# VectorE makes the sum S3 behind the last pair's first gate and S4 behind its last scaling, in place of the other order

## The chip, the core and the metric

One core of one Trainium2 chip runs the kernel. The metric is the device time of one execution in microseconds (us). The engines are TensorE (PE in the profile, PEld its weight loads), VectorE (DVE), ScalarE (ACT), GpSimd (POOL) and SyncE (SP), which issues the DMA transfers of weights.

## The reference, cut to what matters

A trunk of two layers (`DEPTH` 2), width 1024, 512 tokens, all in float32. Each layer mixes tokens and then runs a convolutional feed-forward block, which is where the change lies:

```
h = rmsnorm(x, g_ffn[l])
z = dwconv_centred(h @ w_up[l], conv_w[l], conv_b[l])      # three taps along the tokens
z_gate, z_val = split(z, [D_FF])                            # D_FF = 2816
x = x + (silu(z_gate) * z_val) @ w_down[l]
```

## The kernel before, in words

**Float32 products in three passes.** Every weight slab (128 x 1024, one of a ring of four slots `raw(0)` to `raw(3)`) is split in two: ScalarE writes its high part `w_hi` (a Copy into fp32r), and GpSimd then subtracts it from the slab and writes the low part `w_lo` (`low`, L397 to L399). A product is then three matmuls: high by high, high by low, low by high.

**The feed-forward block** goes through the 22 tiles of D_FF in parts: two full parts of 8 tiles and a last one of 6, in each of the two layers. In a full part the up projection makes two tiles (a pair) in each of four stages, k = 0 to 3 (`up_pair`). TensorE projects four slabs (gate and value of two tiles, accumulators 0 to 3); VectorE multiplies each with the rms scale (`scale(0)` to `scale(3)`, L1204), ScalarE makes the middle tap (`centre`, L738), VectorE adds the two outer taps (`taps`, L1213), ScalarE takes silu, and VectorE gates (`gate`, L1220). ScalarE and VectorE also split the gated tile into high and low parts.

**The down projection of a full part** is done in two quads of four output tiles each, by a Winograd form of Strassen's product: seven products ("units") of half size in place of eight. It needs sums of the weight quarters beside the quarters themselves: S1 = raw(1) + raw(3), S2 = S1 - raw(0), S4 = raw(2) - S2, and S3 = raw(0) - raw(1), which is written over raw(1). It also needs sums T1 to T4 of the activations (`t1` to `t4` in `up_pair`, L1238 to L1251). In the last pair stage (k = 3) of a full part the first quad's weights are prepared: GpSimd makes S1 and S2 (L410, L412), VectorE makes S4 and S3. There are four such stages in the program: two full parts in each of two layers.

**The order around the change** is written out by hand, one instruction stream for each engine, which runs in order, with semaphores between:

- VectorE, stage k = 3: ..., `gate(0)`, S4 (L1232, waits for S2 by `sum_done_pool`), `scale(2)` (L1204), the low part of the even tile (L1235), t1 (L1238), `taps(1, 0)`, the low part of t1 (L1241), `scale(3)`, S3 (L1244), `taps(1, 1)`, `gate(1)`, t2, t4, t3 (L1248 to L1251). Then `down_quads`: it adds unit 1's product to x (`add_unit`, L1264), splits the odd tile and the t's (`odd_low`, L1188 and L1190), adds unit 2, makes the second quad's sums (L1278 to L1290) and adds the other units. Each sum counts up `sum_done`, and the consumers wait for a count and not for a name.
- ScalarE, stage k = 3 (`unit_hi`, L726): high parts of raw(0), S1, S2, raw(2), then `centre(1, 1)`, then S3 (raw(1)) into slot 0, after a wait for unit 1 and for `sum_done`. Then the odd tile and the t's (L791, L792), and in `down_quads` S4 into slot 1 and raw(3).
- GpSimd (`low_quads`, L401 to L424): low(raw(0)), S1, S2, low(S1), then a wait for the high part of S2 and for `sum_done` 6m + 2 (both sums), low(S2), low(raw(2)), low(S3), low(S4), low(raw(3)), and the second quad's seven. With m counting the full parts, `sum_done` rises by six in each.
- TensorE (`down_quads`, L1718 on; matmuls at L1696, L1698, L1699; a unit of all four pairs is 24 matmuls of 256 columns): unit 1, raw(0) by the even tile, into bank 0; unit 2, S1 by T1, into bank 1; the first half of raw(2) by the odd tile (12 matmuls, bank 2), which waits for low(raw(2)) by `lo_sum` 6m + 3; then S2 by T2 into bank 0, which waits for low(S2) and for `unit_added` 6m + 1, that is until VectorE has added unit 1 out of bank 0; its last pair waits for the t's low parts (`t_ready`); the second half of raw(2) by the odd tile; then S4 by the odd tile into bank 1, which waits for low(S4); S3 by T3; raw(3) by T4; and the second quad.
- SyncE reloads raw(0) with the second quad's slab once low(S2) is done (`lo_done`), raw(2) once low(S4) is done. The loads of raw(1) and raw(3) of the second quad went earlier, into other memory.

Of the kernel before, what the change touches and what calls it, by code (L numbers as in the profile page):

```python
# [41 lines left out]
RING = 4  # L42
# [31 lines left out]
def encoder(nc, xT, slabs, rank_w, gate_w, gate_b, spatial_w, spatial_b, ln_gb, gains, gla_gain, conv, consts, outT):  # L74
    with ExitStack() as ctx:
# [187 lines left out]
        def raw(j):  # L263
            return w_raw[:, j * SLAB:(j + 1) * SLAB]
# [107 lines left out]
        @block.gpsimd  # L372
        def _(pool):

            pool.memset(ones, 1.0).then_inc(ones_set, 1)
            pool.memset(eps[:, :], EPS).then_inc(lo_done, RING)
            for j, part in ((0, 0), (1, 0), (0, 1), (1, 1), (0, 2), (1, 2)):
                w = slice(j * SLAB + W_PARTS[part].start, j * SLAB + W_PARTS[part].stop)
                if part < 2:
                    pool.wait_ge(hi_part[j], part + 1)  # L380
                else:
                    pool.wait_ge(hi_done, j + 1)
                pool.tensor_tensor(w_lo[:, w], w_raw[:, w], w_hi[:, w].bitcast(F32),
                                   ALU.subtract).then_inc(lo_part[j] if part < 2 else lo_done, 1)
            pool.wait_ge(xg_ready, KT)
            for j in (2, 3):
                w = slice(j * SLAB, (j + 1) * SLAB)
                pool.wait_ge(hi_done, j + 1)
                pool.tensor_tensor(w_lo[:, w], w_raw[:, w], w_hi[:, w].bitcast(F32),  # L389
                                   ALU.subtract).then_inc(lo_done, 1)  # L390
            def low_slabs(L, first, end):
                with pool.Fori(L * (NS // RING) + first // RING, L * (NS // RING) + end // RING) as q:
                    for j in range(RING):
                        pool.wait_ge(hi_done, q * RING + (j + 1))
                        low(j, raw(j)).then_inc(lo_done, 1)

            def low(slot_of, source):  # L397
                w = slice(slot_of * SLAB, (slot_of + 1) * SLAB)
                return pool.tensor_tensor(w_lo[:, w], source, w_hi[:, w].bitcast(F32), ALU.subtract)  # L399

            def low_quads(L, part):  # L401
                m, slab = quads_at(L, part)
                n = L * NS + slab
                pool.wait_ge(hi_sum, 6 * m + 1)
                low(0, raw(0)).then_inc(lo_sum, 1)
                pool.wait_ge(raw_loaded[1], 16 * (n // RING) + 16)
                pool.wait_ge(raw_loaded[3], 16 * (n // RING) + 16)
                if m:
                    pool.wait_ge(sum_done, 6 * m)
                pool.tensor_tensor(sum_s1, raw(1), raw(3), ALU.add).then_inc(sum_done_pool, 1)  # L410
                pool.wait_ge(sum_done_pool, 2 * m + 1)
                pool.tensor_tensor(sum_s2[:, :], sum_s1, raw(0), ALU.subtract).then_inc(sum_done_pool, 1)  # L412
                pool.wait_ge(hi_sum, 6 * m + 2)
                low(1, sum_s1).then_inc(lo_sum, 1)
                pool.wait_ge(hi_done, n + 1)
                pool.wait_ge(sum_done, 6 * m + 2)
                low(2, sum_s2[:, :]).then_inc(lo_done, 1)
                pool.wait_ge(hi_sum, 6 * m + 3)
                low(3, raw(2)).then_inc(lo_sum, 1)
                pool.wait_ge(hi_done, n + 2)  # L420
                low(0, raw(1)).then_inc(lo_done, 1)
                pool.wait_ge(hi_done, n + 3)
                low(1, sum_s4).then_inc(lo_done, 1)
                pool.wait_ge(hi_done, n + 4)  # L424
                low(2, raw(3)).then_inc(lo_done, 1)

                pool.wait_ge(hi_sum, 6 * m + 4)
                low(3, raw(0)).then_inc(lo_sum, 1)
                pool.wait_ge(hi_sum, 6 * m + 5)
                low(1, sum_s1).then_inc(lo_sum, 1)  # L430
                pool.wait_ge(hi_sum, 6 * m + 6)
                low(0, raw(2)).then_inc(lo_sum, 1)
                pool.wait_ge(hi_done, n + 5)
                pool.wait_ge(sum_done, 6 * m + 6)
                low(2, sum_s2[:, :]).then_inc(lo_done, 1)
                pool.wait_ge(hi_done, n + 6)
                low(3, second_raw[1]).then_inc(lo_done, 1)
                pool.wait_ge(hi_done, n + 7)
                low(1, sum_s4).then_inc(lo_done, 1)
                pool.wait_ge(hi_done, n + 8)  # L440
                low(2, second_raw[3]).then_inc(lo_done, 1)

            for L in range(DEPTH):
                before = RING if L == 0 else 0
                for part in range(FULL_PARTS):
                    low_slabs(L, before, N_FFN + part * PART + 2 * KT)
                    low_quads(L, part)
                    before = N_FFN + (part + 1) * PART
                low_slabs(L, before, NS)
# [3 lines left out]
        def _(act):  # L453
# [91 lines left out]
            with act.Fori(0, DEPTH) as L:  # L545
# [179 lines left out]
                def unit_hi(slot_of, source, done):  # L725
                    act.activation(w_hi[:, slot_of * SLAB:(slot_of + 1) * SLAB], source, ACT.Copy).then_inc(done, 1)  # L726

                def up_pair(slab, tile, stage, even, odd, t_of, down=None):
# [49 lines left out]
                    if down is None:  # L778
                        centre(1, 1)
                        next_hi(3)  # L780
                    else:
                        act.wait_ge(acc_ready, L * NS + slab + RING)
                        raw_at(2, first)
                        unit_hi(3, raw(2), hi_sum)
                        centre(1, 1)
                        act.wait_ge(unit_done, 14 * m + 1)
                        act.wait_ge(sum_done, 6 * m + 2)
                        unit_hi(0, raw(1), hi_done)
                    act.wait_ge(t_done, stage * 2 + 2)
                    on_its_own(act)  # L790
# [3 lines left out]
                def down_quads(part):  # L794
                    m, slab = quads_at(L, part)
                    act.wait_ge(unit_done, 14 * m + 2)
                    unit_hi(1, sum_s4, hi_done)
                    act.wait_ge(unit_done, 14 * m + 3)
                    unit_hi(2, raw(3), hi_done)

                    act.wait_ge(unit_done, 14 * m + 4)
                    raw_at(0, slab + RING)
                    unit_hi(3, raw(0), hi_sum)
                    act.wait_ge(unit_done, 14 * m + 5)
                    act.wait_ge(sum_done, 6 * m + 3)
                    unit_hi(1, sum_s1, hi_sum)
                    act.wait_ge(unit_done, 14 * m + 6)
                    raw_at(2, slab + RING)
                    unit_hi(0, raw(2), hi_sum)
                    act.wait_ge(unit_done, 14 * m + 7)  # L810
                    act.wait_ge(sum_done, 6 * m + 5)
                    unit_hi(2, sum_s2[:, :], hi_done)
                    act.wait_ge(unit_done, 14 * m + 8)
                    unit_hi(3, second_raw[1], hi_done)
                    act.wait_ge(unit_done, 14 * m + 9)
                    act.wait_ge(sum_done, 6 * m + 6)
                    unit_hi(1, sum_s4, hi_done)
                    act.wait_ge(unit_done, 14 * m + 10)
                    act.wait_ge(second_loaded[3], 16 * m + 16)
                    unit_hi(2, second_raw[3], hi_done)  # L820

                    act.wait_ge(unit_done, 14 * m + 11)
                    raw_at(0, slab + 2 * RING)
                    split_hi(0)
                    act.wait_ge(unit_done, 14 * m + 13)
                    raw_at(1, slab + 2 * RING)
                    split_hi(1)
                    act.wait_ge(unit_done, 14 * m + 14)
                    raw_at(2, slab + 2 * RING)
                    split_hi(2)  # L830
                    raw_at(3, slab + 2 * RING)
                    split_hi(3)
# [60 lines left out]
        def _(dve):  # L893
# [49 lines left out]
            with dve.Fori(0, DEPTH) as L:  # L943
# [249 lines left out]
                def up_pair(part, k):  # L1193
# [34 lines left out]
                    gate(0)  # L1228
                    if k == KP - 1:
                        dve.wait_ge(sum_done_pool, 2 * m + 2)  # L1230
                        dve.wait_ge(raw_loaded[2], 16 * (L * (NS // RING)) + 4 * first + 16)
                        dve.tensor_tensor(sum_s4, raw(2), sum_s2[:, :], ALU.subtract).then_inc(sum_done, 1)  # L1232
                    scale(2)
                    dve.wait_ge(feat_hi_done, L * NF + part * KT + (KT + 2 * k + 1))
                    dve.tensor_tensor(lo(0, H), gated[0][:, 0:H], hi(0, H).bitcast(F32),  # L1235
# [5 lines left out]
                    dve.tensor_tensor(lo(H, H), t1, hi(H, H).bitcast(F32), ALU.subtract).then_inc(t_ready, 1)  # L1241
                    scale(3)
                    if k == KP - 1:
                        dve.tensor_tensor(raw(1), raw(0), raw(1), ALU.subtract).then_inc(sum_done, 1)  # L1244
                    taps(1, 1)
                    gate(1)
                    dve.wait_ge(gated_done, f + 2)
# [680 lines left out]
```

## Time and profile before

| | us |
|---|---|
| median of 3 runs | 1109.97 (1109.26 to 1110.15) |
| the profiled execution, its own time | 1112.22 |
| its span in the trace | 1110.3 |
| TensorE busy | 1090.2 |
| VectorE busy | 666.3 |
| ScalarE busy | 516.4 |
| GpSimd busy | 553.8 |

The mean granted clock of TensorE over the span is 0.989 of full speed. The span is what the trace covers; the execution's own time is 1.9 us more. In the rows, a time is the start in us from the span's beginning and the second number is the duration; x2 are two like instructions merged. The record of a GpSimd or VectorE instruction covers the time from its issue to its end, waits inside the instruction included; waits for a semaphore stand as idle time before it. A row of windows has its length, the busy time and count of PE, PEld, DVE, ACT and POOL, TensorE's granted clock as a share of full speed (PEclk), and the DMA share and GB/s.

### The profile page before, as it was taken

The page shows a single profiled execution, that of the slowest core. Times are in us where ns is not written, and L with a number is a line of the kernel's source. Part 1 is how long each engine was busy: PE and PEld are TensorE (multiplying, and loading weights), DVE is VectorE, ACT ScalarE, POOL GpSimd, SP SyncE. Part 2 cuts the span into 40 slices and gives each one's busy share as a digit, 9 for nine tenths or more (in the row PEclk, how much of TensorE's full clock was granted, in tenths as well). Part 3 has the DMA queues.
Part 4 walks back from the last instruction along what each step waited for, and adds up shares of the span by engine and source line. Part 5 has one row for each costly group of instructions (what it writes and reads, how often), then busy time and mean ns, then how long its engine had stood idle before and what let it go on. Part 6 is the DMA issues. An engine that isn't in the chain of part 4 may idle for free.

```text
span 1110.3 us, 17568 instructions
## 1 busy us (share of the span) xinstructions
PE 1090.2 (98%) x5904; PEld 932.7 (84%) x5904; DVE 666.3 (60%) x960; ACT 516.4 (47%) x720; POOL 553.8 (50%) x234
## 2 busy tenths in 40 slices
PE   9999999999899999999999999999989999899997
PEld 7788888888898889888878888888879888898887
DVE  5726755677826777355636368467776377744545
ACT  7835444454434443344557344355443444333441
POOL 5333244345774459644634333334468544685450
PEclk9999999999999999999999999999999999899999
DMA  8222222232142221423522221223322423133222
GB/s 306 86 95 78 76 76 96 78 112 94 40 152 95 94 76 57 152 95 98 178 97 94 78 77 58 95 76 106 103 76 72 138 95 118 46 101 115 95 76 76
DMA packets 33620, 108.96 MB, mean 98 GB/s; under 512 B 3984, under 2 KB 6800, under 8 KB 33552
## 3 DMA queue, kind: packets, MB, share of 16 engines
q1 hardware_dynamic: 32848, 107.03, 29.1%
q10 hardware_dynamic: 704, 1.07, 0.3%
q8 instruction: 38, 0.62, 0.2%
q14 instruction: 30, 0.25, 0.1%
HBM read 105.98 MB, written 2.10 MB: 97 GB/s over the span
## 4 chain that ended last, share of the span: by engine, by line
issue 48%; POOL 32%; PE 14%; DVE 2%; ACT 1%; DMA 1%; POOLq 1%; DVEq 0%; SPq 0%; ACTq 0%
POOL w_lo L399 30%; PE acc L1385 3%; PE acc L1386 3%; PE acc L1387 3%; PE acc L1696 2%; PE acc L1699 2%; PE acc L1698 2%; POOL sum_s L412 1%; POOL mixer_sb L410 1%; DMA x<-xT 1%; DVE arena L1213 1%; DVE arena L1360 1%; DVE side L1204 1%; DVE w_raw L1244 0%; POOL w_lo L389 0%
## 5 line engine op out<-in xcount | busy, mean ns | idle before, releaser
L399 POOL TENSOR_TENSOR w_lo<-w_raw,w_hi 128x1024 fp32r<-128x1024 f32 x180 | 441.0, 2455 | 492.3 <-ACT w_hi L457 468.4
L1385 PE MATMUL acc<-xg_hi,w_hi 128*128 128x512 f32 x864 | 338.9, 392 | 0.0
L1386 PE MATMUL acc<-xg_lo,w_hi 128*128 128x512 f32 x864 | 336.3, 389 | 0.0
L1387 PE MATMUL acc<-xg_hi,w_lo 128*128 128x512 f32 x864 | 336.2, 389 | 0.0
L457 ACT ACTIVATE w_hi<-w_raw 128x1024 fp32r<-128x1024 f32 x158 | 166.7, 1059 | 163.8 <-PE acc L1387 94.7
L1385 PEld LDWEIGHTS acc<-xg_hi,w_hi 128*128 128x128 f32 x864 | 162.2, 188 | 35.6 <-issue 2.0
L1387 PEld LDWEIGHTS acc<-xg_hi,w_lo 128*128 128x128 f32 x864 | 162.2, 188 | 34.0
L1386 PEld LDWEIGHTS acc<-xg_lo,w_hi 128*128 128x128 f32 x864 | 162.3, 188 | 33.3 <-issue 0.5
L1213 DVE SCALAR_TENSOR_TENSOR arena<-side,conv_sb,arena 128x511 f32<-128x511 f32 x128 | 95.9, 749 | 64.8 <-ACT arena L738 54.0
L1385 PE MATMUL acc<-feat_hi,w_hi 128*128 128x512 f32 (+1 forms) x236 | 89.3, 379 | 0.0
L1386 PE MATMUL acc<-feat_lo,w_hi 128*128 128x512 f32 (+1 forms) x236 | 89.3, 378 | 0.0
L1387 PE MATMUL acc<-feat_hi,w_lo 128*128 128x512 f32 (+1 forms) x236 | 89.3, 378 | 0.0
L1696 PE MATMUL acc<-feat_hi,w_hi 128*128 128x256 f32 x256 | 74.4, 291 | 12.2 <-POOL w_lo L399 12.2
L738 ACT ACTIVATE arena<-side,conv_sb 128x512 f32<-128x512 f32 x64 | 49.7, 777 | 74.4 <-DVE side L1204 73.3
L1264 DVE TENSOR_TENSOR x<-x,acc 128x512 f32<-128x512 f32 (+1 forms) x56 | 40.4, 721 | 64.7 <-PE acc L1699 64.7
L1699 PE MATMUL acc<-feat_hi,w_lo 128*128 128x256 f32 x256 | 74.0, 289 | 0.0
L1698 PE MATMUL acc<-feat_lo,w_hi 128*128 128x256 f32 x256 | 73.9, 289 | 0.0
L1696 PEld LDWEIGHTS acc<-feat_hi,w_hi 128*128 128x128 f32 x256 | 50.4, 197 | 13.1 <-POOL w_lo L399 13.0
L1204 DVE TENSOR_TENSOR side<-acc,rstdT 128x512 f32<-128x512 f32 x64 | 44.4, 693 | 27.2 <-PE acc L1387 25.6
L898 DVE SCALAR_TENSOR_TENSOR xg_lo<-x,gains_sb,xg_hi 128x512 fp32r<-128x512 f32 x32 | 40.7, 1280 | 30.0 <-ACT xg_hi L466 29.9
L1696 PE MATMUL acc<-t_hi,w_hi 128*128 128x256 f32 x192 | 57.0, 297 | 0.1
L1698 PE MATMUL acc<-t_lo,w_hi 128*128 128x256 f32 x192 | 56.5, 295 | 0.0
(177 smaller groups left out, 1734.0 us busy)
## 6 DMA issues: line engine op xcount, KB each, us to landing
w_raw<-slabs SPq DMA_DIRECT2D x182, 512.0 KB, 3.3
arena<-slabs SPq DMA_DIRECT2D x8, 512.0 KB, 5.0
outT<-arena SPq DMA_DIRECT2D x7, 256.0 KB, 2.2
mixer_sb<-ln_gb SPq DMA_DIRECT2D x2, 512.0 KB, 7.0
w_raw<-slabs SPq DMA_DIRECT2D x4, 128.0 KB, 4.3
x<-xT ACTq DMA_DIRECT2D x2, 256.0 KB, 4.4
x<-xT SPq DMA_DIRECT2D x2, 256.0 KB, 5.7
x<-xT ACTq DMA_DIRECT2D x1, 512.0 KB, 6.7
```

The source lines that it names most:

```text
L399: return pool.tensor_tensor(w_lo[:, w], source, w_hi[:, w].bitcast(F32), ALU.subtract)
L457: act.activation(w_hi[:, w], w_raw[:, w], ACT.Copy).then_inc(hi_done, 1)
L738: act.activation(z[j], y[j], ACT.Identity, scale=conv_sb[:, bass.ds(coef + 1, 1)], bias=conv_sb[:, bass.ds(coef + 3, 1)]).then_inc(centre_ ...
L898: dve.scalar_tensor_tensor(out=xg_lo[:, w], in0=x[:, w], scalar=gains_sb[:, bass.ds(r * KT + m, 1)], in1=xg_hi[:, w].bitcast(F32), op0=ALU ...
L1204: dve.tensor_tensor(y[j], acc[j][:, :], rstdT[:, :], ALU.mult).then_inc(y_ready, 1)
L1213: dve.scalar_tensor_tensor(out=to, in0=of, scalar=conv_sb[:, bass.ds(coef + tap, 1)], in1=to, op0=ALU.mult, op1=ALU.add).then_inc(taps_don ...
L1385: pe.matmul(out, wh, ah, start=first, stop=False)
L1386: pe.matmul(out, wh, al, start=False, stop=False)
L1387: return pe.matmul(out, wl, ah, start=False, stop=last)
L1696: pe.matmul(out, w_hi[:, a:a + P], xh, start=(first and k == 0 and r == 0), stop=False, skip_group_check=True)
L1698: pe.matmul(out, w_hi[:, a:a + P], xl, start=False, stop=False, skip_group_check=True)
L1699: last = pe.matmul(out, w_lo[:, a:a + P], xh, start=False, stop=(k == KP - 1), skip_group_check=True)
```

## The change

The two sums of the first quad change places on VectorE, and the counts that others wait for follow:

```diff
@@ GpSimd, low_quads
                 pool.wait_ge(hi_done, n + 1)
-                pool.wait_ge(sum_done, 6 * m + 2)
+                pool.wait_ge(sum_done, 6 * m + 1)
                 low(2, sum_s2[:, :]).then_inc(lo_done, 1)
@@ ScalarE, up_pair
                         act.wait_ge(unit_done, 14 * m + 1)
-                        act.wait_ge(sum_done, 6 * m + 2)
+                        act.wait_ge(sum_done, 6 * m + 1)
                         unit_hi(0, raw(1), hi_done)
@@ ScalarE, down_quads
                     act.wait_ge(unit_done, 14 * m + 2)
+                    act.wait_ge(sum_done, 6 * m + 2)
                     unit_hi(1, sum_s4, hi_done)
@@ VectorE, up_pair
                     gate(0)
                     if k == KP - 1:
                         dve.wait_ge(sum_done_pool, 2 * m + 2)
-                        dve.wait_ge(raw_loaded[2], 16 * (L * (NS // RING)) + 4 * first + 16)
-                        dve.tensor_tensor(sum_s4, raw(2), sum_s2[:, :], ALU.subtract).then_inc(sum_done, 1)
+                        dve.tensor_tensor(raw(1), raw(0), raw(1), ALU.subtract).then_inc(sum_done, 1)
                     scale(2)
...
                     scale(3)
                     if k == KP - 1:
-                        dve.tensor_tensor(raw(1), raw(0), raw(1), ALU.subtract).then_inc(sum_done, 1)
+                        dve.wait_ge(raw_loaded[2], 16 * (L * (NS // RING)) + 4 * first + 16)
+                        dve.tensor_tensor(sum_s4, raw(2), sum_s2[:, :], ALU.subtract).then_inc(sum_done, 1)
                     taps(1, 1)
                     gate(1)
```

GpSimd's wait before low(S2) stands for S3 alone after the change: raw(0) is free to be loaded again once S3 has read it.

## Rows read from the trace of the kernel before

**Rows 1.** The page of the profile, busy time of each engine over the span.
```profile
PE 1090.2 (98%) x5904; PEld 932.7 (84%) x5904; DVE 666.3 (60%) x960; ACT 516.4 (47%) x720; POOL 553.8 (50%) x234
```

**Rows 2.** The waits of all engines: who waited for whom, us in total, times, longest.
```profile
PE acc L1696 <- POOL w_lo L399: 12.2, 4, 3.3
...
DVE arena L1213 <- DVE arena L1213: 2.1, 8, 0.5
```

**Rows 3.** Timeline of POOL at the first quads: start us, us, what, idle before.
```profile
271.95 2.39 POOL L399 TENSOR_TENSOR w_lo<-mixer_sb,w_hi 128x1024 fp32r<-128x1024 f32 x1
281.37 2.39 POOL L399 TENSOR_TENSOR w_lo<-sum_s,w_hi 128x1024 fp32r<-128x1024 f32 x1 [7.03 <-DVE w_raw L1244]
283.71 4.71 POOL L399 TENSOR_TENSOR w_lo<-w_raw,w_hi 128x1024 fp32r<-128x1024 f32 x2
288.36 3.12 POOL L399 TENSOR_TENSOR w_lo<-mixer_sb,w_hi 128x1024 fp32r<-128x1024 f32 x1
...
305.59 2.40 POOL L399 TENSOR_TENSOR w_lo<-sum_s,w_hi 128x1024 fp32r<-128x1024 f32 x1
```

**Rows 4.** Timeline of DVE, the same stretch.
```profile
272.25 3.17 DVE L1232 TENSOR_TENSOR mixer_sb<-w_raw,sum_s 128x1024 f32<-128x1024 f32 x1 [1.28 <-POOL sum_s L412]
...
279.06 0.43 DVE L1241 TENSOR_TENSOR feat_lo<-arena,feat_hi 128x256 fp32r<-128x256 f32 x1
279.40 0.69 DVE L1204 TENSOR_TENSOR side<-acc,rstdT 128x512 f32<-128x512 f32 x1
280.00 1.22 DVE L1244 TENSOR_TENSOR w_raw<-w_raw 128x1024 f32<-128x1024 f32 x1
281.35 0.75 DVE L1213 SCALAR_TENSOR_TENSOR arena<-side,conv_sb,arena 128x511 f32<-128x511 f32 x1
...
285.32 0.68 DVE L1264 TENSOR_TENSOR x<-x,acc 128x512 f32<-128x512 f32 x1
...
286.89 2.34 DVE L1190 TENSOR_TENSOR t_lo<-arena,t_hi 128x768 fp32r<-128x768 f32 x1
```

**Rows 5.** Timeline of ACT, the same stretch.
```profile
277.34 1.05 ACT L726 ACTIVATE w_hi<-sum_s 128x1024 fp32r<-128x1024 f32 x1
...
279.50 1.04 ACT L726 ACTIVATE w_hi<-w_raw 128x1024 fp32r<-128x1024 f32 x1
...
286.76 1.05 ACT L726 ACTIVATE w_hi<-mixer_sb 128x1024 fp32r<-128x1024 f32 x1
```

**Rows 6.** Timeline of PE, the same stretch.
```profile
280.12 0.28 PE L1696 MATMUL acc<-feat_hi,w_hi 128*128 128x256 f32 x1
...
282.88 0.28 PE L1699 MATMUL acc<-feat_hi,w_lo 128*128 128x256 f32 x1
286.12 0.38 PE L1696 MATMUL acc<-feat_hi,w_hi 128*128 128x256 f32 x1 [2.97 <-POOL w_lo L399]
...
288.27 0.41 PE L1696 MATMUL acc<-t_hi,w_hi 128*128 128x256 f32 x1
...
293.46 0.28 PE L1696 MATMUL acc<-feat_hi,w_hi 128*128 128x256 f32 x1
...
308.05 0.39 PE L1696 MATMUL acc<-t_hi,w_hi 128*128 128x256 f32 x1
```

**Rows 7.** Windows from TensorE's restart to its S4 unit; PEclk stands behind POOL's busy time.
```profile
286.12:293.46 7.34, 7.34 (x49) 7.34 (x50) 7.26 (x6) 2.74 (x4) 5.47 (x3) 0.77 0.18 51
...
830.57:838.97 8.40, 8.40 (x48) 8.40 (x49) 7.57 (x6) 2.76 (x4) 5.44 (x3) 0.65 0.25 87
...
sum 31.53, PE 31.48 PEld 31.48 DVE 29.80 ACT 10.24 POOL 21.87; mean PE 7.87 PEld 7.87 DVE 7.45 ACT 2.56 POOL 5.47
```

**Rows 8.** Timeline of DVE in an ordinary pair stage of layer 1.
```profile
798.43 2.09 DVE L1241 TENSOR_TENSOR feat_lo<-arena,feat_hi 128x256 fp32r<-128x256 f32 x1
```

**Rows 9.** Timeline of POOL, that same stage.
```profile
797.84 2.40 POOL L399 TENSOR_TENSOR w_lo<-w_raw,w_hi 128x1024 fp32r<-128x1024 f32 x1 [2.93 <-ACT w_hi L457]
```

**Rows 10.** All instructions of line L1241: duration ns min/median/max.
```profile
L1241 DVE TENSOR_TENSOR feat_lo<-arena,feat_hi x16: 424/2088/2109, 213.4 to 956.7; 128x256 fp32r<-128x256 f32 x16
```

## The prediction

> **What bounds the kernel now.** I read the page first: TensorE is busy for 1090.2 us of the span and no other engine comes near [rows 1], so only what makes TensorE stand still, or slows its clock, counts. The list of waits names one large stop that repeats: TensorE's L1696 waits for GpSimd's low parts, four times, 12.2 us in all [rows 2]. These are the four full parts, at the point that the diff touches. The timelines of the first of them, engine by engine, give the chain; the other three show the same order.
>
> TensorE begins unit 2 at 280.12 and issues its last matmul at 282.88, so 24 matmuls take 2.88 us, 0.12 each. It restarts at 286.12 with raw(2) by the odd tile, begins S2 by T2 at 288.27 and S4 by the odd tile at 293.46 [rows 6]. The restart waits for low(raw(2)), the first of the two GpSimd instructions that begin at 283.71; it stands behind low(S2), which began at 281.37 after 7.03 us of idleness that S3 ended [rows 3]. S3 ran on VectorE from 280.00 to 281.22 [rows 4]. The high part of S2 was there from 278.39 (277.34 + 1.05), that of raw(2) from 280.54 [rows 5]. So GpSimd stood still for 3 us for S3 alone.
>
> Behind each stop the clock is low for a while. From restart to the S4 unit TensorE issues 48 matmuls, 5.76 us at 0.12. The first window is 7.34 us at a mean clock of 0.77, the third 8.40 us at 0.65; the four sum to 31.53 [rows 7]. The half clock (1.2 for 2.4 GHz) thus costs 31.53 - 4 x 5.76 = 8.5 us, 1.6 us in two of the parts and 2.6 in the others.
>
> **The change, part by part** (first full part; the others take the same steps).
>
> *S3 moves forward.* It takes S4's place at 272.25. S4 there took 3.17 us [rows 4], since GpSimd's low(S1), 271.95 to 274.34 [rows 3], lay beside it: the S4 record ends at 275.42, which is 274.34 + 1.08. S3 alone takes 1.22, of which some 1.08 is work, and has the same shape, so I cost it at the same 3.17 and `scale(2)` behind it does not move. Bounds: 1.22 and 3.17. Both are hidden, because TensorE is in its up slabs then.
>
> *GpSimd starts low(S2) earlier.* It is released by the high part at 278.39; the step from ScalarE to GpSimd is 0.07 or so, making 278.46 to 280.86 in place of 281.37. The new count asks for S3, which is long done.
>
> *What the earlier start collides with.* L1241 (the low part of t1) reads two SBUF operands, and in this stage it took only 0.43 us, with GpSimd idle [rows 4]. Over all 16 stages its median is 2088 ns, its least 424 [rows 10]. An ordinary stage shows why: GpSimd's instruction begins at 797.84 and ends at 800.24, L1241 begins 0.59 later and ends at 800.52, 0.28 behind it [rows 8, 9]. With low(S2) from 278.46 and L1241 from 279.06 the new stage has the same geometry, so L1241 ends at about 281.14, not 279.49. That is +1.65 for VectorE. It also holds unit 2 of TensorE, which needs that low part, from 280.12 to 281.2.
>
> *S4 moves behind `scale(3)`.* `scale(3)` (0.69, one operand in PSUM, never stretched) runs to 281.75. S4 wants to start at 281.65, but GpSimd has taken up low(raw(2)) at 281.14, and it needs 2.25 once it is free to run: the instruction that begins at 288.36 ends at 291.48, 2.25 behind the end (289.23) of the VectorE instruction that was ahead of it [rows 3, 4]. So low(raw(2)) ends at 283.40, and S4 at 283.40 + 1.08 = 284.48. S3 ended at 281.22 in this place: VectorE's tail is 3.26 us late. Bounds for S4: 1.22 if nothing stood in its way, the 3.17 of rows 4 at the most; worked out it is 2.83, and the latter is the nearer row, since there too GpSimd's instruction was under way.
>
> *What of TensorE's gains.* low(raw(2)) comes at 283.40 in place of 286.05. TensorE ends unit 2 at 281.2 + 2.88 = 284.08 and goes straight on with raw(2) by the odd tile, 12 matmuls, to 285.52. **Then it stops again**: S2 by T2 goes into bank 0 and waits until VectorE has added unit 1 out of it. That add stands behind `taps(1, 1)`, `gate(1)`, t2, t4, t3. Before, it ran 285.32 to 286.00, which was 2.27 before TensorE's S2 unit at 288.27 [rows 4, 6]. With the tail 3.26 late it ends at 289.26, and TensorE restarts at 289.33. The two taps had a gap of up to 0.5 us between them (eight gaps, 2.1 us in all [rows 2]); if that goes, 288.9. I take 289.15.
>
> *The rest of the way to the S4 unit* is 36 matmuls (S2 by T2, and the second half of raw(2)), 4.32 us and the clock's cost c. So S4's unit starts at 289.15 + 4.32 + c = 293.47 + c, and before it was 286.12 + 5.76 + c = 291.88 + c: **+1.6 us a part**, between +1.2 (288.9, the tap gap gone) and +1.8. The new stop, from 285.52 to 289.15, is 3.6 us for 3.1, so I expect no less of the low clock, and take the same 8.5 us for all four. Its ends: 1.6 in each part (6.4 in all) and 2.7 in each (10.8), the two values of rows 7, so -2.1 to +2.3 in all.
>
> *What must not be late behind it.* low(S3) is hidden. S4's high part moves with the odd tile's work on ScalarE, from 286.76 [rows 5] to about 289.8, and low(S4) from 288.36 to 291.0, ended at 293.3: in time for 293.47 + c, as c was never below 1.6. The t's low part (L1190, 2.34 before [rows 4]) finds GpSimd idle and takes about 1 us; it is there by 291.1, when the third pair of S2 by T2 is done. SyncE's reload of raw(0) starts earlier, that of raw(2) about 2 us later, needed only for the second quad's sums some 8 us on. Low parts of the second quad are close: low(S2) there ran 305.59 to 307.99 and TensorE's unit began at 308.05 [rows 3, 6]. Both move back together, so I cost it at nothing, and at 0.5 us a part if one more collision falls there.
>
> **Sum.** 4 x 1.6 = +6.4 us. Against the profiled execution that is 1112.22 + 6.4 = 1118.6, a span of 1116.7. The median of the runs shown is 1109.97, 2.25 below the profiled execution, and the forecast for the median is 1109.97 + 6.4 = 1116.4.
>
> **Rivals.**
>
> *The intended gain arrives (6%).* If L1241 and S4 ran beside GpSimd unhindered, VectorE's tail would stay where it is, the add would end at 286.00 and TensorE would go on at 286.07: 286.07 + 4.32 = 290.4 with a stop of 1.5 us and perhaps no low clock. Against 293.46 that is -3.1 a part, -12.3, about 1097.7. Against it stand rows 8 and 10. The Trainium skill, "Advanced Engine Details and Errata", section VectorE Performance Modes, says that VectorE's 2-port instructions and GpSimd's block each other, and names no others; by that, float32 subtractions would run free and 1097.7 would come out. The Trainium skill, "SBUF — State Buffer", section Who interferes with whom, says that a VectorE instruction with two SBUF inputs contends with a GpSimd one that reads SBUF, and that the first to issue holds the port to its end, which speaks against this change. By that one the sum above stands, and the trace agrees with it: 2.09 against 0.43 us for one and the same L1241.
>
> *S4 slips in ahead of low(raw(2)) (10%).* If GpSimd's queued instruction came second, S4 would end at 282.9, the tail would be 1.65 late, low(raw(2)) would end at 285.1, and TensorE would restart at 287.7: 292.0 + c, +0.1 a part, and from +0.5 us in all to -6 where the shorter stops (2 us) keep the clock up. 1104 to 1110.5. Against it: S4 is asked for half a microsecond after low(raw(2)) can start.
>
> *Slower by more (12%).* The late tail takes with it low(S4), by the ScalarE work between. Its place is the S4 unit; it decides if low(S4) ends behind 293.47 + c, that is if the tail is a further 1.8 us late, as by one more collision of L1190 with a 2.25 us GpSimd instruction. Then each part pays 1 us more, +10 to +11: 1120.5. Together with the clock at its dear value, 1122.
>
> *The change does nothing measurable (4%).* Only if TensorE's wait for bank 0 had as much slack as the tail loses; 2.27 us of slack against 3.26 says no, and the slack was itself the old stop.
>
> **Numbers.** The forecast's own case has 68%: +6.4, from 4 x 1.2 - 2.1 = +2.7 to 4 x 1.8 + 2.3 = +9.5. The range runs from 1111.5 (the lower end of that, with 1 us for an S4 that waits less) to 1121 (its upper end with part of the third rival). About 0.2% (2.2 us) is what a measurement of this kernel can tell from no change. Faster by more: 6% and half of the second rival's 10%, and a little, 0.11. Within: the other half, 4% of no effect, and the forecast's lower tail, 0.10. Slower: 0.79.
>
> **What would show it.** Right: GpSimd's idle time before low(S2) down from 7 to about 4 us and ended by ScalarE; L1241 in all 16 stages near 2.09; L1232 behind `scale(3)` at 2.8 us; L1244 at 3.2; TensorE's wait before L1696 no longer for GpSimd's low part but for VectorE's L1264, on the matmuls of t_hi, 3 to 4 us in each part, with a short one of 1 us before unit 2; low clock still there in all four. Wrong: L1241 at 0.43 with GpSimd running; S4 at 1.2 us; the add of unit 1 at 286; or a clock that no longer falls, which alone would give back 8.5 us and turn the sign.

## The result, and the profile after

The changed kernel takes 1117.49 us in the median of five runs (1114.22 to 1117.81), the kernel before 1109.97 (1109.26 to 1114.32, five runs). The ratio is 1.0056, with a 95% interval from 1.0032 to 1.008: slower by 3.6 to 8.9 us. The profiled execution took 1117.64 us with a span of 1115.9; against that of before it is 5.4 us more, and the span 5.6.

The list of who waited for whom, for TensorE, in the changed kernel (us in all, times, longest). Some lines stand one further on than before: L1697 is the old L1696, L1265 the add (L1264), L1205 a scaling (L1204), L1214 a tap (L1213), L1189 and L1191 the low parts of the odd tile and of the t's (L1188, L1190). L1232 is now S3, and L1245 the moved S4.

```profile
PE acc L1697 <- DVE x L1265: 13.0, 4, 3.4
PE acc L1697 <- DVE feat_lo L1241: 4.1, 4, 1.0
...
PE acc L1697 <- POOL w_lo L399: 0.5, 2, 0.3
```

Against [rows 2], the four waits of 12.2 us for GpSimd's low parts are gone. In their place stand four of 13.0 us for VectorE's add of unit 1 and four of 1.0 us for L1241. TensorE stops for longer than before, and for another engine.

GpSimd's timeline in the first full part, to be read against [rows 3]. The trace of after runs 0.1 us behind that of before at this point.

```profile
278.57 2.39 POOL L399 TENSOR_TENSOR w_lo<-sum_s,w_hi 128x1024 fp32r<-128x1024 f32 x1 [4.13 <-ACT w_hi L726]
280.92 2.57 POOL L399 TENSOR_TENSOR w_lo<-w_raw,w_hi 128x1024 fp32r<-128x1024 f32 x1
283.98 2.84 POOL L399 TENSOR_TENSOR w_lo<-w_raw,w_hi 128x1024 fp32r<-128x1024 f32 x1 [0.49 <-ACT w_hi L726]
291.02 2.37 POOL L399 TENSOR_TENSOR w_lo<-mixer_sb,w_hi 128x1024 fp32r<-128x1024 f32 x1 [4.21 <-ACT w_hi L726]
```

With the offset taken off, low(S2) starts 2.9 us earlier, behind ScalarE's high part, and low(raw(2)) ends at 283.5 in place of 286.05. That is what the diff changes for GpSimd, and it works. VectorE's timeline, against [rows 4]:

```profile
272.12 3.40 DVE L1232 TENSOR_TENSOR w_raw<-w_raw 128x1024 f32<-128x1024 f32 x1 [1.09 <-POOL sum_s L412]
...
279.16 2.07 DVE L1241 TENSOR_TENSOR feat_lo<-arena,feat_hi 128x256 fp32r<-128x256 f32 x1
281.16 0.69 DVE L1205 TENSOR_TENSOR side<-acc,rstdT 128x512 f32<-128x512 f32 x1
281.76 2.81 DVE L1245 TENSOR_TENSOR mixer_sb<-w_raw,sum_s 128x1024 f32<-128x1024 f32 x1
284.50 0.74 DVE L1214 SCALAR_TENSOR_TENSOR arena<-side,conv_sb,arena 128x511 f32<-128x511 f32 x1
...
288.46 0.68 DVE L1265 TENSOR_TENSOR x<-x,acc 128x512 f32<-128x512 f32 x1
...
290.03 0.96 DVE L1191 TENSOR_TENSOR t_lo<-arena,t_hi 128x768 fp32r<-128x768 f32 x1
```

L1241 takes 2.07 us, S4 2.81. Each of the two was asked for while a low part of GpSimd's was under way, and ends 0.3 and 1.1 us behind it (GpSimd's ends are 280.96 and 283.49). The add of unit 1 ends at 289.14, where it ended at 286.00. TensorE's restart, and then its S4 unit:

```profile
289.29 0.36 PE L1697 MATMUL acc<-t_hi,w_hi 128*128 128x256 f32 x1 [3.37 <-DVE x L1265]
...
295.17 0.28 PE L1697 MATMUL acc<-feat_hi,w_hi 128*128 128x256 f32 x1
```

The four windows from that restart to the S4 unit (the last row is their sum; PEclk stands behind POOL's busy time). They hold 36 matmuls, not the 48 of [rows 7].

```profile
289.29:295.17 5.88, 5.88 (x37) 5.88 (x37) 5.83 (x6) 2.72 (x3) 2.58 (x2) 0.71 0.12 18
...
970.72:977.33 6.61, 6.61 (x34) 6.61 (x35) 6.25 (x6) 2.71 (x3) 2.37 (x1) 0.56 0.19 55
sum 24.21, PE 24.20 PEld 24.21 DVE 23.70 ACT 10.86 POOL 9.91; mean PE 6.05 PEld 6.05 DVE 5.92 ACT 2.72 POOL 2.48
```

The half clock costs 24.21 - 4 x 4.32 = 6.9 us in these windows, against 8.5 in the profiled execution of before.

### The profile page after: what moved, and what is told of

It reads as the page before. It is cut to its first block, busy times and chain, and to the rows that moved or that the text cites. A ratio compares the mean times of both kernels' runs of the same rounds, so it can differ in the third digit from the quotient of the medians.

```text
span 1115.9 us, 17572 instructions
## 1 busy us (share of the span) xinstructions
PE 1090.3 (98%) x5904; PEld 932.0 (84%) x5904; DVE 676.5 (61%) x960; ACT 516.4 (46%) x720; POOL 554.8 (50%) x234
## 4 chain that ended last, share of the span: by engine, by line
issue 49%; POOL 31%; PE 13%; DVE 3%; ACT 2%; DMA 1%; POOLq 1%; DVEq 0%; SPq 0%; ACTq 0%
POOL w_lo L399 29%; PE acc L1388 3%; PE acc L1387 3%; PE acc L1386 3%; PE acc L1697 2%; PE acc L1699 1%; PE acc L1700 1%; DVE arena L1214 1%; POOL sum_s L412 1%; POOL mixer_sb L410 1%; DMA x<-xT 1%; ACT arena L738 1%; DVE arena L1361 1%; DVE side L1205 1%; POOL w_lo L389 0%
## 5 line engine op out<-in xcount | busy, mean ns | idle before, releaser
L1214 DVE SCALAR_TENSOR_TENSOR arena<-side,conv_sb,arena 128x511 f32<-128x511 f32 x128 | 95.9, 749 | 64.3 <-ACT arena L738 54.0
L1265 DVE TENSOR_TENSOR x<-x,acc 128x512 f32<-128x512 f32 (+1 forms) x56 | 40.3, 722 | 61.4 <-PE acc L1700 61.1
L1697 PE MATMUL acc<-feat_hi,w_hi 128*128 128x256 f32 x256 | 73.0, 285 | 4.1 <-DVE feat_lo L1241 4.1
L1697 PE MATMUL acc<-t_hi,w_hi 128*128 128x256 f32 x192 | 58.1, 303 | 13.6 <-DVE x L1265 13.0
L1205 DVE TENSOR_TENSOR side<-acc,rstdT 128x512 f32<-128x512 f32 x64 | 44.4, 693 | 27.1 <-PE acc L1388 25.5
L1700 PE MATMUL acc<-t_hi,w_lo 128*128 128x256 f32 x192 | 57.3, 299 | 0.0
```

The lines of the kernel that those rows point to most:

```text
L1205: dve.tensor_tensor(y[j], acc[j][:, :], rstdT[:, :], ALU.mult).then_inc(y_ready, 1)
L1214: dve.scalar_tensor_tensor(out=to, in0=of, scalar=conv_sb[:, bass.ds(coef + tap, 1)], in1=to, op0=ALU.mult, op1=ALU.add).then_inc(taps_don ...
L1697: pe.matmul(out, w_hi[:, a:a + P], xh, start=(first and k == 0 and r == 0), stop=False, skip_group_check=True)
L1700: last = pe.matmul(out, w_lo[:, a:a + P], xh, start=False, stop=(k == KP - 1), skip_group_check=True)
```

## The experiments

Two theories stood at the start. **Port**: L1241 and S4 have both operands in SBUF and wait while a low part of GpSimd's is under way; that makes VectorE's tail late, and TensorE waits for it. **Order**: the new order of the sums is itself what costs. All runs below are timed against the kernel before on the same chip; its medians there were 1109.85 to 1109.92 us, as good as its 1109.97 above. The changed kernel was not timed again beside them: where a run is compared with it, its 1117.49 us are meant. The cuts of diffs are against the changed kernel, or against the kernel before where that is said, and leave out edits that only move a count or a line.

**GpSimd waits for both sums again.**

```diff
 pool.wait_ge(hi_done, n + 1)
-pool.wait_ge(sum_done, 6 * m + 1)
+pool.wait_ge(sum_done, 6 * m + 2)
 low(2, sum_s2[:, :]).then_inc(lo_done, 1)
```

> The changed kernel with one edit: GpSimd waits for both sums again before low(S2), so the order on VectorE is the new one but GpSimd starts as late as before. Port theory (VectorE's L1241 and S4 are stretched because GpSimd is at work beside them, and that makes the tail late): L1241 back at 0.43 us, S4 at 1.22 us behind the second scaling, low(S2) from about 281.4, TensorE's stop of 3 us before raw(2) again, and the time of the kernel before, 1110 us within 2. Rival (the new order by itself costs, through the later S4): 1116 to 1118, as the changed kernel.

Measured: 1109.91 us, ratio to before 1.0006 (0.9996 to 1.0017). Two rows of its VectorE timeline, L1241 and S4:

```profile
278.95 0.43 DVE L1241 TENSOR_TENSOR feat_lo<-arena,feat_hi 128x256 fp32r<-128x256 f32 x1
...
279.89 1.22 DVE L1245 TENSOR_TENSOR mixer_sb<-w_raw,sum_s 128x1024 f32<-128x1024 f32 x1
```

With the new order and the old start of GpSimd, both instructions shrink to 0.43 and 1.22 us and the whole loss is gone. Order falls: the new order by itself costs nothing, and the loss comes with GpSimd's earlier start.

**The add of unit 1 ahead of S4.**

```diff
 scale(3)
 if k == KP - 1:
+    add_unit(0, 0, 0, 0, 14 * m + 1, unit_added)
     dve.wait_ge(raw_loaded[2], 16 * (L * (NS // RING)) + 4 * first + 16)
     dve.tensor_tensor(sum_s4, raw(2), sum_s2[:, :], ALU.subtract).then_inc(sum_done, 1)
...
-add_unit(0, 0, 0, 0, units + 1, unit_added)
```

> The changed kernel with the add of unit 1 moved ahead of S4 on VectorE, where it fits into the time that S4 waits for GpSimd. Tail theory (the add is only the first of several things that come late; the t's low part is next): TensorE starts S2 by T2 at about 285.7 and stops 3 us later in the same unit, before its last pair, for VectorE's low part of the t's (ends near 291.0); 0.4 us a part gained, 1114 to 1117. Rival (the bank alone holds TensorE): the stop goes and 3.4 us a part with it, about 1104 or less.

Measured: 1113.10 us, ratio to before 1.0029 (1.0018 to 1.004). TensorE's waits for VectorE:

```profile
PE acc L1698 <- DVE t_lo L1191: 10.5, 4, 2.6
PE acc L1698 <- DVE feat_lo L1241: 4.2, 4, 1.1
```

The stop moved, it did not go: TensorE now stops for the t's low part, which ends at 290.5. So the bank was only the first of the late things; the tail as a whole is late. (Two waits for GpSimd, 2.2 us in all, came up in second quads besides.) It gained 4.4 us where 0.5 to 3.5 was expected. Part of that is probably the clock: the profile has two stretches of half clock behind these stops where the changed kernel's has four, and of the runs with a mean clock of 0.999 the one of the changed kernel took 1114.22 us and the one of this kernel 1113.03, only 1.2 us less. That is one run of each, so the split stays open.

**S4 made by GpSimd**, in its idle time before low(S2), and no longer by VectorE (those who wait for S3 wait for both sums again, 6m + 2).

```diff
 low(1, sum_s1).then_inc(lo_sum, 1)
+pool.wait_ge(sum_done_pool, 2 * m + 2)
+pool.wait_ge(raw_loaded[2], 16 * (n // RING) + 16)
+pool.tensor_tensor(sum_s4, raw(2), sum_s2[:, :], ALU.subtract).then_inc(sum_done, 1)
 pool.wait_ge(hi_done, n + 1)
-pool.wait_ge(sum_done, 6 * m + 1)
+pool.wait_ge(sum_done, 6 * m + 2)
```

> The changed kernel with S4 made by GpSimd behind low(S1), where GpSimd is idle for 4 us, and no longer by VectorE. Port theory: S4 on GpSimd takes 2.4 us (some 1 us more if it waits for S3 on the port), low(S2) still starts at about 278.6, L1241 still 2.09; VectorE's taps start at about 283.0 when the centre tap is ready and not at 284.5, the add of unit 1 ends near 287.3, TensorE stops for 1.8 us in place of 3.4: 1.9 us a part less, 1110; 1103 if the shorter stop keeps the clock at full speed. Rival (S4's 2.8 us on VectorE is not on the path): 1116 to 1118.

Measured: 1107.63 us, ratio to before 0.9978 (0.9969 to 0.9986), with no half clock behind the stops. Its TensorE waits:

```profile
PE acc L1697 <- DVE x L1265: 6.5, 4, 1.6
PE acc L1697 <- DVE feat_lo L1244: 4.0, 4, 1.0
PE acc L1697 <- POOL w_lo L399: 3.9, 4, 1.0
```

The first line halved as the port theory has it, and the clock stayed up, and yet the time is 1107.6 and not 1103. The third line says where the rest went: a stop of 1.0 us in each *second* quad, where GpSimd's chain of low parts is now the bound. Between 289.8 and 302.9 each of VectorE's four sums meets a low part and takes some 2.9 us:

```profile
289.83 3.01 DVE L1279 TENSOR_TENSOR mixer_sb<-arena 128x1024 f32<-128x1024 f32 x1
...
293.36 2.83 DVE L1282 TENSOR_TENSOR arena<-w_raw,arena 128x1024 f32<-128x1024 f32 x1
```

**Both edits together.** 

> Both edits: S4 on GpSimd, and the add of unit 1 right behind the second scaling, while the centre tap is awaited. Tail theory: S2 by T2 starts at 285.7 without a wait, and TensorE stops before its last pair until about 289.2 (1.4 us); the S4 unit starts near 291.4 in place of 295.2: about 1101 with the clock at full speed behind these short stops, 1108 if it still falls. Rival (bank or port are not what binds): no faster than the S4-on-GpSimd kernel alone.

Measured: 1108.55 us, ratio to before 0.9987 (0.9978 to 0.9995). The stop for the add went (6.5 us to none), one of 5.8 for the t's low part came, and the waits for GpSimd rose to 4.3. No gain beside the run before, but 0.9 us more: the rival named the right outcome. What fits it is that the second quad's chain of low parts sets the time by now, which the next run tests.

**S4's high part earlier on ScalarE**, on top of S4 on GpSimd.

```diff
 unit_hi(0, raw(1), hi_done)
+act.wait_ge(unit_done, 14 * m + 2)
+unit_hi(1, sum_s4, hi_done)
...
-act.wait_ge(unit_done, 14 * m + 2)
-act.wait_ge(sum_done, 6 * m + 2)
-unit_hi(1, sum_s4, hi_done)
```

> The kernel with S4 on GpSimd, and on ScalarE the high part of S4 moved ahead of the odd tile's work (behind a wait for unit 2), so that GpSimd makes low(S4) right behind low(S3), at about 286.4. The kernel with S4 on GpSimd stops 1 us in each second quad, since GpSimd meets four VectorE sums on the port there. Theory: with low(S4) gone from 289.4, the second quad's first sum (L1279) finds GpSimd idle and takes 1.2 us for 3.0, the chain of low parts to low(S2) of the second quad ends 1 us sooner, and that stop goes: about 1103.6. Rival (the chain starts no earlier and keeps its length, since it waits for raw(3)'s high part): 1107.6 as without the edit.

Measured: 1104.58 us, ratio 0.9938 (0.9921 to 0.9955). The second quad's first sum finds GpSimd idle, and TensorE's waits for low parts fall from 3.9 to 0.9 us:

```profile
290.02 1.21 DVE L1278 TENSOR_TENSOR mixer_sb<-arena 128x1024 f32<-128x1024 f32 x1
```

**Slab 3's scaling ahead of L1241**, on top of that.

```diff
+if k == KP - 1:
+    scale(3)
 dve.wait_ge(t_hi_done, stage * 2 + 1)
 dve.tensor_tensor(lo(H, H), t1, hi(H, H).bitcast(F32), ALU.subtract).then_inc(t_ready, 1)
-scale(3)
+if k < KP - 1:
+    scale(3)
```

> As the kernel before it in this call, and in the last pair stage the scaling of slab 3 goes ahead of L1241 on VectorE, so that the 1.65 us that L1241 loses to low(S2) no longer holds the centre tap. Port theory: L1241 still ends with low(S2) near 281.1 and TensorE's 1 us stop before unit 2 stays, but taps start at 281.3 for 283.1, the add of unit 1 ends near 285.6, and the stop before S2 by T2 (1.6 us) goes: about 1.6 us a part less, 1097. Rival (GpSimd's chain in the second quad is the bound by now): 1102 to 1104.

Measured: 1102.21 us, ratio 0.9916 (0.9899 to 0.9934), a miss by 5 us and inside the rival's range, though not for the rival's reason: TensorE's waits for GpSimd were 0.8 us in all. The stop for the add went as expected, but the t's low part (2.20 us, stretched behind low(S4)) came in its place with 3.3 us, and 4.1 us for L1241 stayed.

**TensorE's stop filled**, in the changed kernel (shown) and, in its stop behind unit 2, in the one before: 28 and 24 matmuls that nothing reads.

```diff
+pe.wait_ge(y_ready, ys + 4)
+for _ in range(28):
+    pe.matmul(acc[3][:, 0:H], feat_hi[:, 0:P], feat_hi[:, 0:H], start=True, stop=True, skip_group_check=True)
 pe.wait_ge(lo_done, n + 1)
 pe.wait_ge(unit_added, 6 * m + 1)
```

> The changed kernel with 28 matmuls of 256 columns (3.36 us) that nothing reads, into bank 3, in TensorE's stop of 3.65 us before S2 by T2. Theory of the clock (the stop costs its length, and the half clock behind it as much as 1.6 to 2.3 us a part more): S2 by T2 starts where it did, no half clock behind it, about 6.9 us less, 1110.6. Rival (the half clock is hidden, as other engines set the pace behind the stop): 1117.

> The kernel before with 24 such matmuls (2.88 us) in its stop of 3.1 us behind unit 2. Theory of the clock: 8.5 us less than the profiled run of before showed, 1101.5 to 1103. Rival (hidden): 1110.

Measured: 1114.45 us (ratio 1.0028, 1.0017 to 1.0039) and 1107.83 us (0.9972, 0.996 to 0.9984). No half clock is left behind the stops in either. But the gains are 3.0 and 2.1 us, not 6.9 and 8.5, and neither the theory's forecasts nor the rival's came out. For the kernel before, the 8.5 us are not the right measure: its profiled execution, at a mean clock of 0.989 and 1112.22 us, had more half clock than its usual run, at 0.993 to 0.996. The first experiment has the same stop as the kernel before and was profiled at 0.994. There the four windows of [rows 7] sum to 27.73 us, so the half clock takes 27.73 - 4 x 5.76 = 4.7 us, and the third part has none of it. So the fair pairs are 2.1 of 4.7 us for the usual runs, 1112.22 - 1108.04 = 4.2 of 8.5 us for the two profiled executions, and 3.0 of 6.9 us for the changed kernel: about half each time. The one run of the changed kernel that had a mean clock of 0.999 without any filling took 1114.22 us, as the filled one does. In the filled kernel before, TensorE waits for GpSimd again, for the most part in the second quads:

```profile
PE acc L1696 <- POOL w_lo L399: 4.0, 7, 0.8
```

The profiled execution of before has no such wait behind its four stops. In the changed kernel the same waits rise from 0.5 to 3.9 us by the filling. So about half of what the clock gives back is lost to GpSimd's chain of low parts; at half clock TensorE is late enough not to wait for it.

**One wait added to the changed kernel.** GpSimd lets L1241 pass before it starts low(S2).

```diff
 pool.wait_ge(sum_done, 6 * m + 1)
+pool.wait_ge(t_ready, 2 * KP * (m + 1) - 1)
 low(2, sum_s2[:, :]).then_inc(lo_done, 1)
```

> The changed kernel with one wait more: GpSimd starts low(S2) only when L1241 of this stage is done. Port theory: an added wait makes it faster. L1241 takes 0.43 us, low(S2) runs 279.6 to 281.95, S4 (asked for at 280.1) ends at 283.0 and not 284.5, low(raw(2)) ends near 285.3, the add of unit 1 near 287.8, and TensorE restarts with S2 by T2 near 287.9 for 289.3: about 1.4 us a part less, 1111 to 1113. Rival (GpSimd's low parts set TensorE's pace there, so that holding them back costs): 1118 or more.

Measured: 1109.23 us, ratio to before 0.9992 (0.9984 to 1.0001), so 8 us faster than the changed kernel, by waiting longer, and no faster than the kernel before. L1241 and S4:

```profile
279.65 0.42 DVE L1242 TENSOR_TENSOR feat_lo<-arena,feat_hi 128x256 fp32r<-128x256 f32 x1
...
280.59 3.15 DVE L1246 TENSOR_TENSOR mixer_sb<-w_raw,sum_s 128x1024 f32<-128x1024 f32 x1
```

It came out 2 us better than the range. In its trace low(raw(2)) ran behind S4 and ended at 286.0, and TensorE stopped for that, which hid the late add (in three of the four parts; in the third it still waited 0.8 us for it). Three stretches of half clock were left, of 2.6 to 3.2 us, where the changed kernel has four, three of 2.8 to 3.2 us and one of 5.3. How the 2 us divide between the two was not tested.

**The same wait, with S4 on GpSimd and its high part early.** 

> S4 on GpSimd and its high part early, and GpSimd yielding to L1241 as in the kernel before it in this call. Port theory: TensorE's stop before unit 2 (1.0 us) goes and one of about 1.3 us before raw(2) by the odd tile comes; the add of unit 1 ends near 285.8; then it depends on who asks first, L1191's low part of the t's (near 286.9) or low(S4) (near 286.7): 1104 to 1105 if low(S4) holds the port, 1100 if not. Rival (yielding only shifts the stop): 1104.6 as without it.

Measured: 1100.75 us, ratio 0.9912 (0.9898 to 0.9926). The t's low part asked before low(S4) (at 286.45, and it took 1.06 us):

```profile
PE acc L1697 <- POOL w_lo L399: 8.5, 8, 1.3
```

Nothing of VectorE holds TensorE any more; two short stops for low parts are left in each full part.

**The second quad's S3 earlier**, on top of the 1102 us kernel, without the added wait.

```diff
 dve.tensor_tensor(sum_s1, second_raw[1], second_raw[3], ALU.add).then_inc(sum_done, 1)
-add_unit(0, 0, 1, 0, units + 3, unit_added)
 dve.wait_ge(raw_loaded[0], loads)
+dve.wait_ge(sum_done, 6 * m + 3)
 dve.tensor_tensor(second_raw[1], raw(0), second_raw[1], ALU.subtract).then_inc(sum_done, 1)
+add_unit(0, 0, 1, 0, units + 3, unit_added)
```

> The 1102 us kernel (S4 on GpSimd, its high part early, scaling of slab 3 ahead of L1241) with the second quad's S3 made right behind its S1 on VectorE, before the add of S2 by T2, while GpSimd is idle. Theory: that sum then starts at 290.8, ahead of GpSimd's next low part at 291.4, and takes 1.2 us for 3.4; GpSimd's chain in the second quad loses only half a microsecond there, so TensorE's waits for it (0.8 us in all) go: 1101.2 to 1102. Rival (no change): 1102.2, since the stops before unit 2 and before the t's low part (7.4 us in all) are elsewhere.

Measured: 1100.86 us, ratio 0.9913 (0.9899 to 0.9928). That sum takes 1.23 us and TensorE's waits for GpSimd's low parts in the full parts are gone, as expected; those for VectorE's (4.1 us for t1's low part, 3.3 for the t's) stay:

```profile
290.88 1.23 DVE L1284 TENSOR_TENSOR arena<-w_raw,arena 128x1024 f32<-128x1024 f32 x1
```

These last two beat both kernels, by 9 us the one before and by over 16 the changed one. Their gain is made of work taken off VectorE's late tail and of collisions avoided.

## Why the prediction was right

The forecast was 1116.4 with 1111.5 to 1121; measured was 1117.5. Point by point, by its own steps, in the first full part (0.1 us taken off for the trace's offset):

- *S3 in S4's place costs nothing.* Right: it is stretched to 3.40 (3.17 forecast; it starts 0.2 earlier and ends at the same point), and `scale(2)` behind it does not move.
- *low(S2) from 278.46.* 278.47.
- *L1241 ends at 281.14.* 281.13. TensorE waits 1.0 us for it and starts unit 2 at 281.28 (281.2 forecast; 280.12 before). Over all 16 stages L1241's least is now 2072 ns.
- *S4 2.83 us, ending at 284.48.* 2.81, ending at 284.47.
- *TensorE restarts at 289.15* (between 288.9 and 289.33). 289.19. I had halved the gap between the two taps; in this part it stayed at 0.5, and in the second it was 0.27. With the gap whole my sum gives 289.33. It was 0.14 too late, because I took the tail to be as late as S4's end (3.26 us), but before the change the first tap began 0.13 behind S3's end and now it begins 0.07 before S4's record ends, so the taps, and the add with them, are only 3.0 us late. The two small errors nearly cancelled: that much is luck.
- *+1.6 us a part to the S4 unit, without the clock.* The S4 units start at 295.17, 429.00, 842.58 and 977.33, before at 293.46, 426.15, 838.98 and 972.13: 5.2 us later by the fourth. The clock's part of that is 6.9 - 8.5 = -1.6 us. The trace's offset (0.1) and TensorE's two waits for low parts in second quads (0.5, below) are in it too. That leaves 5.2 + 1.6 - 0.1 - 0.5 = 6.2 us, 1.55 a part.
- *low(S4) in time, from 288.36 to 291.0 and ended at 293.3.* 290.92 to 293.29, ahead of the S4 unit at 295.07.
- *The half clock, 8.5 us as before.* 6.9, inside the -2.1 to +2.3 stated, and there in all four parts of the profile; one of the five timed runs, with a mean clock of 0.999, can have had next to none.
- *The second quad's low parts at nothing.* TensorE waited for them twice, 0.5 us in all, both before the fourth S4 unit. The span is 5.6 us longer; the 0.4 us that come behind that unit stand in no wait that the list names.

In the profiles the difference is thus 5.4 (1117.64 - 1112.22) for the 6.4 forecast: 6.2 for the four parts, 1.6 less by the clock, 0.5 more by the second quads' waits, and a rest of 0.3. In the medians it is 7.5. That gap has a cause that I had not seen. The kernel before has 71 runs timed beside the experiments: 54 have a mean granted clock of 0.993 to 0.996 and take 1108.9 to 1110.7 us, 8 have 0.989 and take 1111.9 to 1112.5, 9 have 0.986 and 1113.7 to 1114.1. The profiled execution of before, with 0.989, is of the middle kind, and its 8.5 us of half clock are more than a usual run has. The changed kernel has 0.990 or 0.991 in four of its five runs, and 0.999 in the fifth, which took 1114.22. So where I took the clock's cost of the profiled execution over to both, the usual run before had less of it: 4.7 us by the first experiment's profile, where the changed kernel's profile has 6.9. With the half clock out of the way in both kernels (the two filled ones) the difference is 1114.45 - 1107.83 = 6.6 us, near the forecast's +6.4. So the mechanism and its price are right, and the term for the clock, zero in my sum, is what was mis-sized: -1.6 us between the two profiles, and in the medians some 1 us the other way (an estimate: half of 6.9 - 4.7, as half of it was lost above).

The Trainium skill, "SBUF — State Buffer", section Who interferes with whom, has the rule that decided it: a VectorE instruction with two SBUF inputs contends with a GpSimd one that reads SBUF, and the order of issue decides who blocks. The traces agree with it: the same L1241 takes 0.43 us beside an idle GpSimd and 2.07 beside a busy one, and whichever asks first goes first. The narrower statement that I had set against it, that of the Trainium skill, "Advanced Engine Details and Errata", section VectorE Performance Modes, gave 1097.7, and lost. The contention works the other way round too: low(S3), asked for at 283.98 while S4 was under way, took 2.84 us and not 2.4.

What one cannot read off the experiments is whether an S4 that slips in ahead of low(raw(2)), with low(S2) as early as in the changed kernel, would have saved what the second rival gave it. The kernel with the added wait comes near (S4 ran ahead of low(raw(2)), 1109.23 us), but there low(S2) began later and S4 waited for it.

## What to carry to other kernels

When two engines share a port, a start that a change brings forward has to be checked against what it will run beside, and not only for whether its inputs are ready: here low(S2) began 2.9 us earlier, and VectorE's add of unit 1 came 3.0 us later for it. A wait or a reordering that lets a short, late instruction pass first can then make the whole faster (one added wait won the changed kernel's 8 us back), and here moving the sum to the engine that idled was better than moving it along the busy one (1107.6 us against 1117.5). And a stall taken away shows what stands behind it: here the bank's add, then the t's low part, then the second quad's low parts, 0.8 to 3.4 us a part each.

## What the runs showed of the hardware that I had not expected

- The half clock costs far less than its stretch suggests where another engine's chain stands close behind: taking it away gave about half of what it held, 4.2 us of 8.5 between the two profiled executions before the change and 3.0 of 6.9 after it.
- One kernel has distinct times, and its runs' mean clocks go with them: medians of 1109.8, 1112.2 and 1113.9 us for the kernel before, at mean clocks of about 0.994, 0.989 and 0.986. That the difference lies behind the same four stops is shown for one pair of profiles alone (8.5 us at 0.989, 4.7 at 0.994 in the first experiment, which has the same stop). So the clock of a profiled execution is to be set beside that of the timed runs before its half clock is put into a sum. Kernels whose stops were at most 1.6 us long had 0.998 or 0.999 in their profiles and times that agree within 0.8 us (1107.50 to 1107.95 over 11 runs, 1100.62 to 1100.97 over 6, 1108.14 to 1108.92 over 11).
